# A two-layer hybrid backbone step: attention ends laid over the projections, and another order of the first layer's mixer

## The reference

```
layer 0:  u, v, gate, xr = split(h @ w_in)                       # 512 columns each
          ya = gelu(u) * (ws @ rmsnorm(gelu(v)) + bs)            # gMLP over chunks of 128 tokens
          r, i = sigmoid(conv(xr) @ wa + ba), sigmoid(conv(xr) @ wi + bi)    # for both directions
          a = exp(8 r log_sigmoid(lam));  h_t = a h_{t-1} + sqrt(1 - a^2) (i * conv(xr))
          yb = (h_forward + h_backward) * gelu(gate)
          y = concat(ya, yb) @ w_out
layer 1:  q, k, v = split(h @ w_qkv);  rope on latent tokens
          y = windowed grouped-query attention(q, k, v, sink) @ w_out
both:     x = x + mod2 * rmsnorm(y);  x = x + mod5 * rmsnorm(relu(h' @ w1)^2 @ w2)
          mod0..mod5 = silu(c) @ w_mod + b_mod, shift and scale ahead of each half
```

## Time and profile before

| what | value |
|---|---|
| median of three runs | 1608.98 us |
| the profiled execution's own time | 1612.72 us |
| its span in the trace | 1610.4 us |
| PE busy | 1496.5 us, 93% |
| DVE, ACT, POOL busy | 657.9, 550.0, 512.2 us |
| mean granted clock of PE | 0.969 |

### The profile page before, as it was taken

One profiled execution on the slowest core, in us unless ns is written; L12 is line 12 of the kernel. 1 busy time (PEld: TensorE's weight loads), 2 busy tenths in 40 slices (PEclk: granted clock), 3 DMA queues, 4 the chain that ended last, 5 costly groups with the idle time before them and its releaser, 6 DMA issues.

```text
span 1610.4 us, 20091 instructions
## 1 busy us (share of the span) xinstructions
PE 1496.5 (93%) x8338; PEld 1241.8 (77%) x8338; DVE 657.9 (41%) x1128; ACT 550.0 (34%) x910; POOL 512.2 (32%) x219
## 2 busy tenths in 40 slices
PE   4899979899999999999789789989899999999998
PEld 3786646787898899897667656657699889989985
DVE  4475663632323222232834466624532222223225
ACT  4347723631131232222531265524532223222311
POOL 1322133243143243232324134413343324323330
PEclk8999979999999999999899899999899999999999
DMA  9313434234343222134142000034232122213221
GB/s 340 125 53 107 155 101 161 66 118 156 109 154 106 79 80 77 55 103 157 51 164 79 27 1 1 1 105 131 81 116 79 54 77 80 78 55 103 79 81 76
DMA packets 90546, 153.87 MB, mean 96 GB/s; under 512 B 6404, under 2 KB 44752, under 8 KB 90456
## 3 DMA queue, kind: packets, MB, share of 16 engines
q1 hardware_dynamic: 82432, 145.76, 27.4%
q10 hardware_dynamic: 8024, 6.83, 1.5%
HBM read 149.69 MB, written 2.89 MB: 95 GB/s over the span
## 4 chain that ended last, share of the span: by engine, by line
PE 41%; DVE 4%; ACT 3%; DMA 1%; issue 1%; POOL 1%; DVEq 0%; ACTq 0%; SPq 0%
PE PS L1223 11%; PE PS L1224 11%; PE PS L1225 11%; PE PS L1497 2%; PE PS L1489 1%; PE PS L1467 1%; PE PS L1450 1%; PE PS L1275 1%; POOL WL L893 1%; PE PS L1468 1%; DVE RAW L537 1%; DVE GG L1188 1%; ACT WH L663 1%; ACT GG L850 1%; DMA RAW<-in_w_mod 1%
## 5 line engine op out<-in xcount | busy, mean ns | idle before, releaser
L893 POOL TENSOR_TENSOR WL<-RAW,WH 128x1024 fp32r<-128x1024 f32 x170 | 418.0, 2491 | 754.5 <-ACT WH L663 754.5
L1223 PE MATMUL PS<-HH,WH 128*128 128x384 f32 (+1 forms) x1152 | 360.2, 313 | 12.5 <-DVE HL L1046 7.9
L1224 PE MATMUL PS<-HL,WH 128*128 128x384 f32 (+1 forms) x1152 | 358.4, 311 | 0.0
L1225 PE MATMUL PS<-HH,WL 128*128 128x384 f32 (+1 forms) x1152 | 357.9, 311 | 0.0
L663 ACT CAST WH<-RAW 128x1024 fp32r<-128x1024 f32 x170 | 168.3, 1046 | 484.9 <-PE PS L1225 338.5
L1223 PE MATMUL PS<-WH,AH 128*128 128x512 f32 x640 | 251.8, 393 | 7.8 <-DVE ACC L1144 7.8
L1225 PE MATMUL PS<-WH,AL 128*128 128x512 f32 x640 | 250.4, 391 | 0.0
L1224 PE MATMUL PS<-WL,AH 128*128 128x512 f32 x640 | 250.3, 391 | 0.0
L1223 PEld LDWEIGHTS PS<-HH,WH 128*128 128x128 f32 x1152 | 221.1, 192 | 17.9 <-issue 10.7
L1224 PEld LDWEIGHTS PS<-HL,WH 128*128 128x128 f32 x1152 | 221.1, 192 | 0.8 <-issue 0.3
L1225 PEld LDWEIGHTS PS<-HH,WL 128*128 128x128 f32 x1152 | 220.9, 192 | 0.0
(11 more groups left out here) (173 smaller groups left out, 1549.2 us busy)
## 6 DMA issues: line engine op xcount, KB each, us to landing
RAW<-in_w_mod SPq DMA_DIRECT2D x43, 1024.0 KB, 5.2
RAW<-in_w_ffn_in SPq DMA_DIRECT2D x32, 1024.0 KB, 5.6
RAW<-in_w_ffn_out SPq DMA_DIRECT2D x32, 1024.0 KB, 4.8
RAW<-in_w_in_even SPq DMA_DIRECT2D x7, 1024.0 KB, 5.4
RAW<-in_w_qkv SPq DMA_DIRECT2D x6, 1024.0 KB, 5.3
RAW<-in_w_out_even SPq DMA_DIRECT2D x4, 1024.0 KB, 5.4
RAW<-in_w_out_odd SPq DMA_DIRECT2D x4, 1024.0 KB, 5.1
X<-in_x_sample SPq DMA_DIRECT2D x4, 512.0 KB, 6.2
```

What stands on the lines that cost most here:

```text
L893: nc.gpsimd.tensor_tensor(ring_view(WL, ld, j), w_view(ld, b), ring_view(WH, ld, j).bitcast(f32), ALU.subtract).then_inc(w_lo, 1)
L1223: MM(out, wh, xh, start=first, stop=False)
L1224: MM(out, wh, xl, start=False, stop=False)
L1225: return MM(out, wl, xh, start=False, stop=last)
```

## The change

**Mixer.** After the two xr pairs come the v and u steps at once, with the `rg` halves of tiles 0 to 2, their `root` steps and three `mod` steps between them. The transpose of the spatial weights (`wst`, before a part of `vnorm`) moves behind the first v step, the square root of v's norm (`vroot`) behind u 0, `vnorm` behind u 1. Gate 0 and 1 come after the last u step, then `gmlp`, `rg` of tile 3, the fourth `mod`, two `ya`, `root(3)`, and gate 2 and 3 just ahead of `wout`. DVE now multiplies with the gate; POOL only adds. yb and ya are split into buffers of their own (`YBH`, `YBL`, `YAH`, `YAL`), ya by DVE alone. The first `wout` step takes ya's four rows first and waits for yb's remainders row by row.

**Attention.** `Q(0)` comes after the second tile of the last query block, units 0 and 1 after the third and the fourth (`around`), and their weights lie in places of their own (`weights_of`). At the end the first two `wout` steps come ahead of `PV(18)` and `PV(19)`, around `sums(19)`; each first `wout` step waits only for its own tile's units. The two `mod` steps of this stage stand behind tiles 2 and 3, where they stood behind 0 and 2.

```diff
-    apair("gate", 0, ("w_in",), 1024)
-    for d in (0, 1):
-        step("rg", uses_a=2, tile=0, d=d)
-    step("root", tile=0)
-    apair("gate", 2, ("w_in",), 1024 + 256)
-    halves = [(1, 0), (1, 1), None, (2, 0), (2, 1), None, (3, 0), (3, 1)]
+    after = {("v", 0): [(rg, 0, 0)], ("v", 1): [(rg, 0, 1), (mod, *fill[0])], ("v", 2): [(root, 0)], ("v", 4): [(rg, 1, 0)],
+             ("u", 0): [(rg, 1, 1), (step, "vroot"), (mod, *fill[1])], ("u", 1): [(root, 1)], ("u", 2): [(rg, 2, 0), (mod, *fill[2])],
+             ("u", 3): [(rg, 2, 1)], ("u", 4): [(root, 2)]}
...
+    ld = load("acols", src=("w_in",), col=1024)
+    ld2 = load("acols", src=("w_in",), col=1024 + 256)
+    apair("gate", 0, ("w_in",), 1024, None, ld)
     step("gmlp", uses_a=4)
-    step("ya", uses_m=1, t=0)
-    step("ya", uses_m=1, t=1)
+    for d in (0, 1):
+        rg(3, d)
+    mod(*fill[3])
+    for t in (0, 1):
+        step("ya", uses_m=1, t=t)
+    root(3)
     flush()
+    apair("gate", 2, ("w_in",), 1024 + 256, None, ld2)
...
+            if nb == 1 and t == 1:
+                unit("Q", 0, uses_m=1)
+            if nb == 1 and t in (2, 3):
+                around(t - 2)
...
+    for i in range(2, last + 1):
+        around(i)
+    j0 = bload(("w_out_odd",), 0)
+    wout(0, 0, j0, pt=True)
+    unit("sums", last)
+    wout(0, 1, j0, pt=True)
+    for i in (last - 1, last):
         unit("PV", i, uses_m=1)
...
-            if nb == 0 and t in (0, 2):
-                mod(1, 2, t // 2)
+            if nb == 0 and t in (2, 3):
+                mod(1, 2, t - 2)
...
+        def weights_of(i):
+            if i < NKV:
+                return GGF[:, 2048 + 512 * i:2560 + 512 * i].rearrange("p (h n) -> p h n", h=4)
+            return Z[:, i % 2, :, :]
+        def gate_of(tile):
+            return GT[:, 3, :] if tile < 2 else XC[tile - 2]
...
# ACT, gate
-                            nc.scalar.activation(GT[:, tile, :], a_bank(a), ACT.Gelu_apprx_tanh).then_inc(a_free[a % 2], 1)
+                            if tile == 1:
+                                act.wait_ge(yb_made, 1)
+                            elif tile > 1:
+                                act.wait_ge(xc_used, 8)
+                            nc.scalar.activation(gate_of(tile), a_bank(a), ACT.Gelu_apprx_tanh).then_inc(a_free[a % 2], 1)
...
+                    for tile in (s["tile"], s["tile"] + 1) if s["what"] == "gate" else ():
+                        act.wait_ge(yb_made, tile + 1)
+                        nc.scalar.copy(YBH[:, tile, :], GT[:, tile, :]).then_inc(yb_hi, 1)
# DVE, gate
+                    if s["what"] == "gate":
+                        pair = (s["tile"], s["tile"] + 1)
+                        for tile in pair:
+                            upto(dve, a_free, s["a"] + tile - pair[0])
+                            dve.wait_ge(h_sum, tile + 1)
+                            V_.tensor_tensor(GT[:, tile, :], GT[:, tile, :], gate_of(tile), ALU.mult).then_inc(yb_made, 1)
+                        for tile in pair:
+                            dve.wait_ge(yb_hi, tile + 1)
+                            V_.tensor_tensor(YBL[:, tile, :], GT[:, tile, :], YBH[:, tile, :].bitcast(f32), ALU.subtract).then_inc(yb_lo, 1)
# POOL, root
-                    nc.gpsimd.tensor_tensor(TH[0], TH[0], TH[1], ALU.add).then_inc(h_sum, 1)
-                    pool.wait_ge(h_sum, j + 1)
-                    nc.gpsimd.tensor_tensor(GT[:, j, :], GT[:, j, :], TH[0], ALU.mult).then_inc(rg_done, 1)
+                    nc.gpsimd.tensor_tensor(GT[:, j, :], TH[0], TH[1], ALU.add).then_inc(h_sum, 1)
# PE, wout
-                            pe.wait_ge(mix_lo, 4)
...
+                        if what == "wout" and s["ph"] == 1 and kt < 4:
+                            tok = (YAH[:, t, P * kt:P * kt + P], YAL[:, t, P * kt:P * kt + P])
+                        elif what == "wout" and s["ph"] == 1:
+                            if nb == 0 and t == 0:
+                                pe.wait_ge(yb_lo, kt - 3)
```

More of the change, by code:

```diff
@@ L203, in schedule @@
             bgroup(what, nb, t, j)
[L204 to L213, removed]
-    step("gmlp", uses_a=4)
-    step("ya", uses_m=1, t=0)
-    step("ya", uses_m=1, t=1)
+            if (what, t) == ("v", 0):
+                step("wst", uses_m=1)
+            for act_, *spec in after.get((what, t), []):
+                act_(*spec)
+            if (what, t) == ("u", 1):
+                step("vnorm")
+    ld = load("acols", src=("w_in",), col=1024)
+    ld2 = load("acols", src=("w_in",), col=1024 + 256)
+    apair("gate", 0, ("w_in",), 1024, None, ld)
+    step("gmlp", uses_a=4)
+    for d in (0, 1):
[4 more added lines that the diff above has]
+    root(3)
     flush()
+    apair("gate", 2, ("w_in",), 1024 + 256, None, ld2)
     for nb in (0, 1):
@@ L232, in schedule, with unit, around @@
     step("l1in")
+    units = [(g, t) for t in range(TT) for g in range(NKV)]
+    last = len(units) - 1
+    def unit(kind, i, **uses):
+        step(kind, n=i, g=units[i][0], t=units[i][1], **uses)
+    def around(i):
+        unit("S", i)
+        if i < last:
+            unit("Q", i + 1, uses_m=1)
+        if i > 1:
+            unit("PV", i - 2, uses_m=1)
+        if i:
+            unit("sums", i - 1)
+        unit("softmax", i)
     k_use = None
@@ L252, in schedule, with wout @@
             step("rope", nb=nb, t=t, group=group, pu=k_use - 1 if nb == 2 and t > 2 else None)
+            if nb == 1 and t == 1:
+                unit("Q", 0, uses_m=1)
+            if nb == 1 and t in (2, 3):
+                around(t - 2)
         if nb == 2:
             step("kvout", group=group - t)
[L255 to L271, removed]
+    for i in range(2, last + 1):
+        around(i)
+    def wout(nb, t, j, **spec):
+        bgroup("wout", nb, t, j, ph=3)
+        steps[-1].update(spec)
+    j0 = bload(("w_out_odd",), 0)
[3 more added lines that the diff above has]
+    for i in (last - 1, last):
         unit("PV", i, uses_m=1)
     for nb in (0, 1):
-        j = bload(("w_out_odd",), nb)
-        for t in range(TT):
-            bgroup("wout", nb, t, j, ph=3)
-            if nb == 0 and t in (0, 2):
-                mod(1, 2, t // 2)
+        j = bload(("w_out_odd",), nb) if nb else j0
+        for t in range(2 - 2 * nb, TT):
+            wout(nb, t, j)
+            if nb == 0 and t in (2, 3):
+                mod(1, 2, t - 2)
             if nb == 0 and t == 4:
@@ L479, in hybrid_step @@
         KT_M = [s["m"] for s in STEPS if s["kind"] == "kT"][-1]
-        GATE_A = [s["a"] + i for s in STEPS if s["kind"] == "A" and s["what"] == "gate" for i in (0, 1)]
         SHEET_M = [s["m"] for s in STEPS if s["kind"] == "sheet"][0]
@@ L1473, in _ @@
                     base = pv_steps(i)
+                    if i == TT * NKV - 2:
+                        for b in EARLY_OUT:
+                            upto(pe, b_free, b)
                     u = s["m"]
```

86 lines of the change are left out of this document (49 added, 37 removed).

## The result

The changed kernel takes 1600.65 us (median of five runs, 1597.03 to 1601.68) beside 1610.62 for the kernel before in the same series: ratio 0.9927 with a 95% interval of 0.9909 to 0.9946, that is 8.7 to 14.6 us gained. A second series of the same kernel gave 0.9936 (0.9917 to 0.9955). Forecast were 25 us and 1584. The time lies inside the range, 1567 to 1603, but the gain is 9 to 15 us and not 25.

The account below looks back on a forecast made before the run. The matrix engine's queue, busy 93% of the span, was taken as the bound. Gains of 12.5 (mixer), 8.9 (attention's start) and 3.6 (attention's end) sum to 25.0 us, giving 1584 us, range 1567 to 1603.

Parts of the forecast that it names:

- The mixer: From the last xr tile to the first wout step: 22.3 us late in place of 34.8, a gain of 12.5 us.
- u 0: First u step in the mixer: waits for its third and fourth weight blocks from POOL, 3.8 us late (bounds 0 and 5).
- the handover: Mixer, gate 1 through gmlp to rg of tile 3: DVE's first product with the gate comes late, 9.6 us in all.
- yb's last rows: First wout step of the mixer: the last two yb rows come 3.3 us late (bounds 0 and 10).
- the clock: Mixer, mod, ya and the start of gate 2 at half clock: 4 us (0 to 14).
- Sum 117.9 us. So 34.8 us are waits or lost clock: Mixer: PE's full-clock work summed from single durations, 117.9 of 152.7 us elapsed; the other 34.8 are waits or lost clock.
- Attention's start: From Q(0) to S(3): earlier query and first units cover latencies, a gain of 8.9 us (bounds 5 and 12).
- 8 + 4.9 = 12.9: Attention's start: 8 us of work plus S(3) 4.9 late, behind PV(0)'s copy waiting for w_out blocks, in place of 21.8.
- Attention's end: From PV(17) through the wout steps: 6.4 us gained, 1.1 and 1.7 given back, net 3.6 us (bounds 1 and 8).
- Full cover: Rival: new mixer waits don't arise, DVE finishes root(2) when gate 1 ends; 45 us gained, 1564 us; chance 0.18.
- The rival in which the vector engine becomes the bound: Mixer: each of root's products and scans waits for a whole POOL block; 12 us gained overall, 1597 us; chance 0.24.
- The slower case: Rival: waits put both mixer gate pairs at half clock, 28 us more, 1612 us; chance 0.05.

Follow-up runs that it names:

- the kernel with the ring: The changed kernel with attention's transposed softmax weights in two idle slots of the weight ring instead of the raw buffer; 1596.66 us, 0.9919 of before.
- the kernel with one early step: The changed kernel with one wout step instead of two ahead of PV(18) and PV(19), mod steps behind tiles 1 and 2; 1597.29 us, 0.9923 of before.

## Why the prediction was wrong in size

**The mixer, 12.5 us forecast, 5.2 found (7.3 in A, 2.1 lost again in B; 4.0 in the second profile).** The list of late items was nearly right: forecast 22.3 us, found 22.5, of it 15.2 of waits and 7.3 lost to the clock. Item by item: v 4's bank 0.2 (1.0 forecast), u 0 2.8 (3.8), the handover 4.9 + 1.2 + 1.1 = 7.2 (9.6), yb's last rows 4.0 (3.3), the clock 7.3 (4.0). The step that failed is the first one, "Sum 117.9 us. So 34.8 us are waits or lost clock". Taking PE's busy time in each microsecond times its granted clock and adding over A gives the work at full clock: 123.0 us before, 122.9 after, 122.5 to 123.2 in four other kernels. The sum of single instructions' durations missed 5.1 us of it: the `B` steps have 62.5 us (59.8 in the sum), the `rg` halves 16.2 (14.9), `gmlp` 4.7 (3.7); gates, `mod` and transposes are within 0.1 of theirs. So only 29.7 us were late before, and 22.5 after: 7.2 us, which is what A gained. I could have had that figure from the profile before. The second term is B: behind the new 4.0 us wait PE runs `ya` and the next `mod` at half clock, and small waits follow, 2.1 us that no line of the forecast had.

**Attention's start, 8.9 forecast, 6.3 found (5.8 in the second profile).** The wait at PV(0) was forecast at 4.5 to 5 us and is 4.42. In C, waits and lost clock fell from 9.9 + 5.0 to 5.8 + 2.4 us. The term that was too small is the 4.9 in "8 + 4.9 = 12.9": it counted the wait alone. Behind it S(3) and Q run at half clock (2.4 us), and other waits take 1.4. The same stop also held DVE, which the kernel with the ring showed: the pair of w_out blocks is the cause in either form.

**Attention's end, 3.6 forecast, 0.4 found (0.0 in the second profile).** At PV(19) the gain is the forecast one: 15.05 + 10.87 - 20.01 = 5.9 us. The give-back up to the first step of the second block was forecast at 2.8 and is 1.2 - 0.4 for the mod weights plus 2.0 - 0.2 for POOL's blocks, 2.6. What failed is that I stopped there: the load of w1 and what hangs on it were put at nothing. PE reaches wout's second block 5.1 us earlier against PV(17) than before (49.5 and 54.6 in the table of the kernel with one early step). There its step waits for POOL's blocks, and ACT, which stood 7.05 us for w1's load, copies the step 1.5 us behind PE. At the copy 1.2 of the 5.1 us are left, at the MLP's first product 0.7. From that copy on one tile of the closing norms takes DVE and ACT 6.3 us, just what PE takes, so PE can't catch up: it waits 2.3 us ahead of the MLP's first product, where it waited 0.4 before. In the experiments I first took PV(19) for the cause, which comes 6.1 us later against PV(17) (20.0 in place of 13.9). The kernel with the ring refutes that: its loads don't wait for PV(19), and w1 is as late. With one early step and the mod steps one tile earlier the loads come 6 to 7 us earlier, PV(18) waits as little (0.8 us), and the whole gain arrives at the MLP (5.6 us at the second block, 5.7 at its first product).

**The rivals.** Full cover is out: DVE was not through. The rival in which the vector engine becomes the bound gave 3 + 7 + 2 = 12 us; found were 5.2 + 6.3 + 0.4 = 11.9. That the sums agree is luck in part, since each of its three terms is off by 0.7 to 2.2 us. Its mechanism is there, DVE's products and scans waiting for whole blocks of POOL, but in `root(3)` four of the eight wait for one (two scans and two products, 2.6 to 3.3 us each), not all eight. The stretch with an eighth of POOL's work shows that POOL's blocks cost the mixer 14 to 16 us, so this rival should have had a larger chance. The slower case did not occur: gate pairs ran at full clock. DVE's load was stated as 75 us in 118; it is busy 107 in 145.4, of which 21.9 are the stretching.

**What was to be seen.** Right: no sigmoid waits in v and u; 2.8 us at u 0; the largest wait of the mixer at `gmlp`, ended by DVE through ACT's gelu; yb's remainder in the first wout step; 4.4 us at PV(0); 0.8 us at PV(18). The mixer's stretch, 145.4, is inside 130 to 150.

The Trainium skill, "ScalarE: Activation LUTs", section "What ACT_TABLE_LOAD costs", would have charged a drain with each table load: after the load at 166.77 us of 1.28 the next activation starts at 168.06, 0.01 us behind, so the trace shows none here either.

## What to carry to other kernels

Before pricing waits one by one, take the work of a stretch from the windows (busy time times granted clock) and not from a sum of single durations; the difference to the elapsed time is all that a reorder can win. A give-back is followed until the engine that sets the pace of the next stage has caught up. Where DVE's chains are short, look which POOL instruction runs beside them: moving it gained 5.7 us in one stretch here and lost 4.7 in the next, and cutting it in pieces gained 5 us in one kernel and nothing in another, so both have to be measured over the whole kernel. When a wait is blamed on one semaphore, take that semaphore's wait out and see whether the time moves.

## What the runs showed of the hardware

- An operation of DVE that reads two operands from SBUF and starts while POOL's tensor_tensor runs is done only behind it, however small: 128x4 took 2.30 us in place of 0.15, a scan 2.51 in place of 0.42. In the changed kernel 39 operations start beside one of POOL's remainders, and all end 0.02 to 1.09 us behind it; ten others that read one operand from PSUM all end ahead of it. The time lost falls with the length of POOL's instruction (21.9, 19.2 and 12.1 us in A with one, two and four pieces). The Trainium skill, "Trainium Architecture — The Big Picture", section "What this means for kernel authors", calls the port that the two share "an exclusive lock (not a bandwidth split)"; the runs agree, and DVE stands for the rest of POOL's whole instruction.
- Cutting a 128x1024 remainder into four costs POOL 0.78 us (2.504 to 3.288), into two 0.30.
- Two profiles of one kernel differed by 7.4 us in span, 5.4 of it where no edit lies. A gain of a few us is to be read from stretches, or from five rounds, not from a pair of spans.
